# More combined feed-forward pairs, with their weight sums and input combinations made elsewhere

## The chip, the cores and the metric

One core of a Trainium2 chip runs the whole program in one launch. The metric is the time of an execution in microseconds, as the median of three runs. All arithmetic is float32. Matrix products go through TensorE's fp32r format, which keeps fewer bits than float32, so each operand is split in a high and a low half and each product is made three times: high x high, high x low, low x high.

## What is computed

Two transformer blocks over 512 positions of width 1024. The first: a norm, an mLSTM with four heads beside a dilated window attention with 24 heads, gates, an output projection (`out`), then a feed-forward. The second: gated linear attention beside sparse attention, `out2`, then a feed-forward. Both feed-forwards have 2816 hidden columns, that is 22 blocks of 128:

```
h = rmsnorm(x, g)                 # x * r * g, with r = rsqrt(mean(x*x) + 1e-6), one r per position
x = x + (silu(h @ w_gate) * (h @ w_up)) @ w_down      # block 2 norms the feed-forward's output before adding
```

## The kernel before

The activations lie transposed in SBUF: `XT` is 8 slabs of 128 features by 512 positions. The weights come from HBM as a fixed list of some 318 units. A unit makes one block of 128 output columns: 8 slabs of 128x128 weights against 8 slabs of 512 positions, three matmuls each, 24 matmuls of 512 columns.

One order of work is written by hand as a Python program (`program`, L1112). It is played once for each engine, with a class per engine that issues that engine's part of each step and does nothing for the rest. So each engine has one queue, in the order of the program, and the engines meet through semaphores only. SP's queue issues the loads.

`unit(e, i)` (L442) is the normal step. `ahead(e, i)` (L416) comes first: `split` of unit i+2 makes its weights' high half on ScalarE (L2064) and the low half on VectorE (L2467), for some units on GpSimd (L3267), and `load` fetches unit i+5 to one of three raw buffers `RAW`. High and low halves (`WH`, `WL`) have three buffers each. Then come the products (L1561 to L1563), then `evict`, which takes the sum out of PSUM. In the out projection `evict` is: VectorE adds the sum to XT (L2655), ScalarE makes the high half AH of XT times the norm's gain and the square, VectorE makes the low half AL (L2446), GpSimd sums the squares (L3258). The norm's factor r, spread as `RB`, is known only after all eight; so `lead` (L456) starts the first three feed-forward units (gate 0 and up 0 in turns, then gate 1) on the unscaled input, and VectorE multiplies their sums by RB when it evicts them (L2613).

From block 8 on in both feed-forwards (`PAIR_FROM`) two gate units, or two up units, are made together as a **pair** by a Strassen-Winograd scheme (`ffn_pairs`, L807). The weights of the two blocks and the two halves of the depth are four chunks a11, a12, a21, a22 of 128x512; seven products replace eight. The chunks are a11, a12, a22 and four sums s1 to s4 of them. VectorE makes the sums in place in `RAW` (L2478 to L2490, `chunk_add`). A product is 12 matmuls of 256 columns (L1637 to L1639). The other side of each product is one of seven combinations of the input's position halves and depth halves, made once per feed-forward for each slab m of four: `forms_x` scales slabs m and m+4 of XT by gain and RB (L2510), `forms` makes four sums (L2523 to L2530), `forms_hi` the high halves on ScalarE (L2078), `forms_lo` the low halves, 1024 of 1792 columns on VectorE (L2536) and the rest on GpSimd (L3282). They are issued one of these pieces per half unit, while units up 1 to up 7 run. The seven products are then put together from PSUM by VectorE (L2544 to L2563); the gate goes through silu on ScalarE and is multiplied with up (L2569). Units of `down` stand between the pairs from block 8 on. In block 1's feed-forward four PSUM banks turn, and a pair takes four.

## Time and profile before

| | before |
|---|---|
| median of 3 runs | 1911.11 us (1911.08 to 1911.13) |
| span of the profiled execution, first to last instruction | 1909.1 us |
| TensorE busy | 1898.5 us, 99% |
| VectorE busy | 1255.4 us, 66% |
| ScalarE busy | 735.3 us, 39% |
| GpSimd busy | 265.1 us, 14% |
| moved by DMA | 172.77 MB, 90 GB/s |

The profiled execution has no time of its own beside its span; the runs' median is 2.0 us above the span. Busy time is the time in which an engine has an instruction running; a matmul's record is longer than its distance to the next one, for matmuls overlap. In lines of a profile, L with a number is a line of the kernel, `out<-in` names what is written and read, and what stands in brackets or behind the bar is the idle time of the engine before the instruction and what ended it. AR is the common name of a large area that many tiles share.

### The profile page before, as it was taken

Reading aid. Unit: us, or ns where it says so; the run is one execution under the profiler, and the core shown is the slowest. Engines: PE = TensorE matmul, PEld = TensorE weight load, DVE = VectorE, ACT = ScalarE, POOL = GpSimd, SP = SyncE. Lnnn points to the kernel's source line nnn. Section 1 sums busy time; section 2 is a strip of 40 time slices with the busy share of each in tenths; the row PEclk is TensorE's granted clock in tenths of the full one; section 3 lists DMA queues with packets and bytes.
Section 4 is the critical chain, followed back from the end, with each engine's and each line's share of the span. In section 5 each row is a group of like instructions: output and inputs, shape, how many; then the busy total and the mean of one; then the engine's idle time right before and its main releaser. Section 6 shows DMA issues by size and latency. Waiting matters only on the chain.

```text
span 1909.1 us, 26308 instructions
## 1 busy us (share of the span) xinstructions
PE 1898.5 (99%) x10599; PEld 1591.0 (83%) x10599; DVE 1255.4 (66%) x1894; ACT 735.3 (39%) x1265; POOL 265.1 (14%) x156
## 2 busy tenths in 40 slices
PE   9999999999999999999999999999999999999998
PEld 7788888888888888999997778877777878899998
DVE  7777543345455748777776756766776667887874
ACT  6332322233334444344435522224444354444442
POOL 0211210111111113000004001121111133100002
PEclk9999999999999999999999999999999999999999
DMA  5322233232321323233333222322121322333332
GB/s 177 102 70 85 88 86 115 89 99 67 89 67 45 115 91 104 78 106 102 114 108 103 77 67 78 100 79 65 56 67 40 116 79 87 100 100 100 100 130 81
DMA packets 53472, 172.77 MB, mean 90 GB/s; under 512 B 5963, under 2 KB 10643, under 8 KB 53352
## 3 DMA queue, kind: packets, MB, share of 16 engines
q1 hardware_dynamic: 52912, 170.66, 28.8%
q8 instruction: 84, 1.38, 0.3%
q10 hardware_dynamic: 440, 0.44, 0.1%
q14 instruction: 36, 0.29, 0.1%
HBM read 168.86 MB, written 2.22 MB: 90 GB/s over the span
## 4 chain that ended last, share of the span: by engine, by line
PE 94%; DVE 3%; ACT 1%; POOL 1%; issue 0%; DVEq 0%
PE PS L1561 22%; PE PS L1563 22%; PE PS L1562 22%; PE PS L1637 5%; PE PS L1639 5%; PE PS L1638 5%; PE PS L1983 1%; PE PS L2005 1%; PE PS L1780 1%; PE PS L1795 1%; PE PS L1961 1%; PE PS L1841 1%; PE PS L1827 1%; PE PS L1818 1%; PE PS L1748 1%; POOL XT L3338 1%
## 5 line engine op out<-in xcount | busy, mean ns | idle before, releaser
L1561 PE MATMUL PS<-HH,WH 128*128 128x512 f32 x1124 | 444.0, 395 | 0.8 <-DVE WL L2467 0.7
L1563 PE MATMUL PS<-HH,WL 128*128 128x512 f32 x1124 | 438.0, 390 | 0.0
L1562 PE MATMUL PS<-HL,WH 128*128 128x512 f32 x1124 | 437.4, 389 | 0.0
L2064 ACT ACTIVATE WH<-RAW 128x1024 fp32r<-128x1024 f32 (+2 forms) x256 | 261.1, 1020 | 336.4 <-PE PS L1563 271.4
L2467 DVE TENSOR_TENSOR WL<-RAW,WH 128x1024 fp32r<-128x1024 f32 (+2 forms) x195 | 251.2, 1289 | 113.7 <-ACT WH L2064 112.0
L1561 PE MATMUL PS<-AH,WH 128*128 128x512 f32 x816 | 323.7, 397 | 0.0
L1563 PE MATMUL PS<-AH,WL 128*128 128x512 f32 x816 | 318.1, 390 | 0.0
L1562 PE MATMUL PS<-AL,WH 128*128 128x512 f32 x816 | 317.6, 389 | 0.0
L1561 PEld LDWEIGHTS PS<-HH,WH 128*128 128x128 f32 x1124 | 211.1, 188 | 49.7 <-issue 4.2
L1563 PEld LDWEIGHTS PS<-HH,WL 128*128 128x128 f32 x1124 | 211.0, 188 | 45.1
L1562 PEld LDWEIGHTS PS<-HL,WH 128*128 128x128 f32 x1124 | 211.2, 188 | 42.2 <-issue 0.2
L3267 POOL TENSOR_TENSOR WL<-RAW,WH 128x1024 fp32r<-128x1024 f32 (+1 forms) x61 | 139.0, 2279 | 740.1 <-ACT WH L2064 740.1
L1637 PE MATMUL PS<-AR,WH 128*128 128x256 f32 x784 | 219.6, 280 | 0.0
L1639 PE MATMUL PS<-AR,WL 128*128 128x256 f32 x784 | 218.8, 279 | 0.0
L1638 PE MATMUL PS<-AR,WH 128*128 128x256 f32 x784 | 218.8, 279 | 0.0
L1561 PEld LDWEIGHTS PS<-AH,WH 128*128 128x128 f32 x816 | 153.2, 188 | 37.1 <-issue 6.5
L1563 PEld LDWEIGHTS PS<-AH,WL 128*128 128x128 f32 x816 | 153.2, 188 | 33.0
L1562 PEld LDWEIGHTS PS<-AL,WH 128*128 128x128 f32 x816 | 153.4, 188 | 30.5 <-issue 0.5
L2613 DVE TENSOR_TENSOR AR<-PS,RB 128x512 f32<-128x512 f32 (+2 forms) x117 | 84.3, 723 | 134.5 <-PE PS L1563 128.0
L2073 ACT ACTIVATE WH<-RAW 128x512 fp32r<-128x512 f32 x196 | 119.4, 624 | 93.3 <-DVE RAW L2486 36.7
L1637 PEld LDWEIGHTS PS<-AR,WH 128*128 128x128 f32 x784 | 147.2, 188 | 1.1
L1638 PEld LDWEIGHTS PS<-AR,WH 128*128 128x128 f32 x784 | 146.7, 187 | 1.1
(360 smaller groups left out, 2260.7 us busy)
## 6 DMA issues: line engine op xcount, KB each, us to landing
RAW<-wst SPq DMA_DIRECT2D x292, 512.0 KB, 3.6
RAW<-wst SPq DMA_DIRECT2D x16, 256.0 KB, 2.6
RAW<-wst SPq DMA_DIRECT2D x8, 384.0 KB, 3.1
XT<-xT SPq DMA_DIRECT2D x3, 512.0 KB, 7.3
out<-XT SPq DMA_DIRECT2D x4, 384.0 KB, 2.5
AR<-mx SPq DMA_DIRECT2D x4, 256.0 KB, 6.2
AR<-scr SPq DMA_DIRECT2D x16, 64.0 KB, 4.3
AR<-scr SPq DMA_DIRECT2D x8, 128.0 KB, 4.8
```

What stands on the lines that cost most here:

```text
L1561: T.matmul(out, wh, XH[:, k, :], start=k == 0, stop=False)
L1562: T.matmul(out, wh, XL[:, k, :], start=False, stop=False)
L1563: m = T.matmul(out, wl, XH[:, k, :], start=False, stop=k == nk - 1)
L1637: T.matmul(out, wh[:, w], xh, start=m == 0, stop=False)
L1638: T.matmul(out, wh[:, w], xl, start=False, stop=False)
L1639: t = T.matmul(out, wl[:, w], xh, start=False, stop=m == 3)
L1748: t = T.transpose(PS[:, b, q * 128:(q + 1) * 128], src[:, q * 128:(q + 1) * 128], ident())
L2064: t = A.activation(whole(WH, i, n), raw(i)[:, 0:n], ACT.Copy, scale=1.0)
L2073: t = A.activation(chunk(WH, i, c), raw_chunk(i, c), ACT.Copy, scale=1.0)
L2467: t = V.tensor_tensor(whole(WL, i, n), raw(i)[:, 0:n], f(whole(WH, i, n)), ALU.subtract)
L2613: return V.tensor_tensor(dst, src, rb, ALU.mult)
L3267: t = G.tensor_tensor(whole(WL, i, n), raw(i)[:, 0:n], f(whole(WH, i, n)), ALU.subtract)
```

## The change

1. `PAIR_FROM` becomes 2 in the first feed-forward and 6 in the second: 20 and 16 pairs, where there were 14 and 14.
2. The weight sums s1 to s4 of all 36 pairs are made ahead by GpSimd. SP loads the two units of a pair (2 x 512 KB) to a new buffer SG (two of them), GpSimd makes the four sums, SP stores them to a tensor in HBM (1 MB). A plan by unit numbers (`sums_ahead`) says when: the first feed-forward's during the mLSTM, the attention and its gates (units 17 to 94), the second's during the first feed-forward.
3. A pair's seven chunks are then loaded one by one, 256 KB each, into half buffers of RAW, each as soon as the low half of the chunk six before is made. VectorE's `chunk_add` goes.
4. The combinations are made of x times gain, without RB. The gate sums of a pair are multiplied by RB on GpSimd (`pair_factor`), go through silu, and are multiplied by RB once more on GpSimd, which stands for the factor of the up sums.
5. In the first feed-forward the four pieces of slab m are issued together behind the eviction of out unit m+4. In the second they start at once behind the lead, one piece per half unit.
6. `forms_lo` makes all 1792 columns on VectorE.

```diff
-PAIR_FROM = 8
+PAIR_FROM = {"": 2, "2": 6}
...
+def sums_ahead():
+    plan, g = {}, AT["gate", 2, 0]
+    ahead_of = {"": list(range(17, 41, 4)) + list(range(42, 57, 3)) + list(range(57, 93, 4)),
+                "2": list(range(g - 8 if PAIR_FROM["2"] < 6 else g, g + 64, 4))}
+    for sfx, at in ahead_of.items():
+        for first, n in zip(at, [n for n, i in enumerate(PAIRS) if UNITS[i][0] in ("gate" + sfx, "up" + sfx)]):
+            last = 6 if sfx else 5
+            for step, what in ((0, "load"), (2, "s1"), (3, "s2"), (3, "s4"), (last - 1, "s3"), (last, "store")):
+                plan.setdefault(first + step, []).append((what, n))
+    return plan
...
 def ahead(e, i):
...
+    sums_on(e, i)
...
     for j in range(8):
         unit(e, unit_of("out", j))
+        if j > 3:
+            for f in (e.forms_x, e.forms, e.forms_hi, e.forms_lo):
+                f("", j - 4)
...
-    forms = [(f, m) for m in range(4) for f in (e.forms_x, e.forms, e.forms_hi, e.forms_lo, e.none)]
+    forms = [(f, m) for m in range(4) for f in (e.forms_x, e.forms, e.forms_hi, e.forms_lo)] if sfx else []
...
+            def load_piece(s, i, c):
+                for key in R_BEFORE[i, c]:
+                    sp.wait_ge(*at(*key))
+                if CHUNKS[c] in SUM_AT:
+                    n, o = PAIRS.index(i), SUM_AT[CHUNKS[c]]
+                    sp.wait_ge(*at("sum", "stored", n))
+                    src = sums_d[n, :, o:o + 512]
...
+            def sum_store(s, n):
+                sp.wait_ge(*at("sum", "s3", n))
+                sp.wait_ge(*at("sum", "s4", n))
+                S.dma_start(sums_d[n, :, :], SG[:, n % 2, :]).then_inc(*sum_out[n % 2].next("sum", "stored", n))
...
             def forms_x(s, sfx, m):
                 g = "fpre2" if sfx else "ffn_g"
-                dve.wait_ge(*at("free", "spread", "n5" if sfx else "n2"))
+                dve.wait_ge(*(at("free", "spread", "n5") if sfx else at("free", "sum", unit_of("out", m + 4))))
...
                 def scaled(dst, j, a, b):
-                    return V.scalar_tensor_tensor(out=dst, in0=XT[:, j, a:b], scalar=col(g, j), in1=RB[:, a:b],
-                                                  op0=ALU.mult, op1=ALU.mult)
+                    return V.tensor_scalar(dst, XT[:, j, a:b], col(g, j), None, ALU.mult, ALU.bypass)
...
             def forms_lo(s, sfx, m):
                 a = 1792 * m
                 dve.wait_ge(*at("forms", "hi", sfx, m))
-                t = V.tensor_tensor(TL[sfx][:, a:a + 1024], TF[:, 0:1024], f(TH[sfx][:, a:a + 1024]), ALU.subtract)
+                t = V.tensor_tensor(TL[sfx][:, a:a + 1792], TF, f(TH[sfx][:, a:a + 1792]), ALU.subtract)
...
+            def sum_add(s, n, what):
+                g = SG[:, n % 2, :]
+                s2, s4, s1, s3 = (g[:, o:o + 512] for o in (0, 512, 1024, 1536))
+                if what == "s1":
+                    pool.wait_ge(*at("sum", "raw", n, 0))
+                    pool.wait_ge(*at("sum", "raw", n, 1))
+                    t = G.tensor_tensor(s1, s1, s3, ALU.add)
...
+            def pair_factor(s, i, n):
+                pool.wait_ge(*at("free", "sum", i + n))
+                pool.wait_ge(*at("free", "spread", norm_of(UNITS[i][0])))
+                t = G.tensor_tensor(GATE[n], GATE[n], RB, ALU.mult)
...
+            def pair_silu(s, i, n):
+                pool.wait_ge(*at("silu", i + n))
+                t = G.tensor_tensor(GATE[n], GATE[n], RB, ALU.mult)
```

## Rows read from the trace of the kernel before

**Rows 1.** The page: busy time of the engines (share of the span) and instructions.
```profile
PE 1898.5 (99%) x10599; PEld 1591.0 (83%) x10599; DVE 1255.4 (66%) x1894; ACT 735.3 (39%) x1265; POOL 265.1 (14%) x156
```

**Rows 2.** The page: chain that ended last, share of the span by engine.
```profile
PE 94%; DVE 3%; ACT 1%; POOL 1%; issue 0%; DVEq 0%
```

**Rows 3.** Waits of TensorE: line waited for, us in total, times, longest.
```profile
PE PS L1539 <- DVE VT L2426: 1.5, 1, 1.5
...
PE PS L1561 <- DVE WL L2467: 0.7, 1, 0.7
```

**Rows 4.** TensorE in time, first combined pair: start us, us, engine, line, count.
```profile
776.51 0.28 PE L1637 MATMUL PS<-AR,WH 128*128 128x256 f32 x1
...
786.29 0.28 PE L1639 MATMUL PS<-AR,WL 128*128 128x256 f32 x1
...
786.41 0.40 PE L1561 MATMUL PS<-HH,WH 128*128 128x512 f32 x1
```

**Rows 5.** VectorE in time, end of the out projection and the lead of block 1.
```profile
672.45 0.69 DVE L2655 TENSOR_TENSOR XT<-XT,PS 128x512 f32<-128x512 f32 x1 [0.97 <-PE PS L1563]
...
673.93 0.75 DVE L2446 SCALAR_TENSOR_TENSOR AL<-XT,COL,AH 128x512 fp32r<-128x512 f32 x1 [0.79 <-ACT AH L2048]
...
677.89 0.69 DVE L2655 TENSOR_TENSOR XT<-XT,PS 128x512 f32<-128x512 f32 x1 [0.97 <-PE PS L1563]
...
691.79 1.45 DVE L2467 TENSOR_TENSOR WL<-RAW,WH 128x1024 fp32r<-128x1024 f32 x1 [0.79 <-ACT WH L2064]
...
700.39 1.23 DVE L2467 TENSOR_TENSOR WL<-RAW,WH 128x1024 fp32r<-128x1024 f32 x1 [7.15 <-ACT WH L2064]
```

**Rows 6.** TensorE in time: first product of gate 1 in block 1.
```profile
700.35 0.39 PE L1561 MATMUL PS<-AH,WH 128*128 128x512 f32 x1
```

**Rows 7.** ScalarE and GpSimd in time: the square of out 4, its sum.
```profile
673.80 0.62 ACT L2054 ACTIVATE AR<-XT 128x512 f32<-128x512 f32 x1
...
674.50 1.34 POOL L3258 TENSOR_TENSOR AR<-AR 128x512 f32<-128x512 f32 x1 [4.10 <-ACT AR L2054]
```

**Rows 8.** VectorE in time: combinations of the first slab, as they run now.
```profile
715.37 0.48 DVE L2510 SCALAR_TENSOR_TENSOR AR<-XT,COL,RB 128x256 f32<-128x256 f32 x1
...
716.16 0.75 DVE L2510 SCALAR_TENSOR_TENSOR AR<-XT,COL,RB 128x512 f32<-128x512 f32 x1
...
717.96 0.42 DVE L2523 TENSOR_TENSOR AR<-AR,VT 128x256 f32<-128x256 f32 x1
...
719.21 0.42 DVE L2530 TENSOR_TENSOR AR<-AR 128x256 f32<-128x256 f32 x1
```

**Rows 9.** Groups by line and shape: high halves; low halves; a weight sum.
```profile
L2078 ACT ACTIVATE AR<-AR 128x1792 fp32r<-128x1792 f32 x8 | 13.6, 1696 | 4.8 <-DVE AR L2530 4.8
...
L2536 DVE TENSOR_TENSOR AR<-AR,AR 128x1024 fp32r<-128x1024 f32 x8 | 9.8, 1222 | 0.9 <-ACT AR L2078 0.6
...
L2482 DVE TENSOR_TENSOR RAW<-RAW 128x512 f32<-128x512 f32 x28 | 19.2, 685 | 0.0
```

**Rows 10.** A VectorE tensor_scalar with two SBUF sides: duration ns, min/median/max.
```profile
L2730 DVE TENSOR_SCALAR AR<-AR,COL x16: 543/547/2300, 30.1 to 200.6; 128x512 f32<-128x512 f32 x16
```

**Rows 11.** GpSimd and VectorE in time: two operations that meet.
```profile
740.70 1.87 POOL L3299 TENSOR_TENSOR AR<-AR,RB 128x512 f32<-128x512 f32 x1 [4.16 <-ACT AR L2150]
...
741.67 1.97 DVE L2467 TENSOR_TENSOR WL<-RAW,WH 128x1024 fp32r<-128x1024 f32 x1 [0.27 <-ACT WH L2064]
```

**Rows 12.** Stretches: busy us of PE, PEld, DVE, ACT, POOL; PEclk, DMA share, GB/s.
```profile
4.00:8.00 4.00, 4.00 (x13) 3.12 (x12) 2.04 (x3) 2.94 (x5) 0.00 (x0) 1.00 1.03 387
900.00:950.00 50.00, 50.00 (x360) 47.08 (x359) 40.38 (x67) 21.55 (x37) 0.00 (x0) 1.00 0.30 96
1903.00:1904.00 1.00, 0.59 (x3) 0.17 (x1) 1.00 (x1) 0.37 (x1) 0.67 (x1) 1.00 0.47 167
1908.00:1909.00 1.00, 0.00 (x0) 0.00 (x0) 0.00 (x0) 0.00 (x0) 0.00 (x0) 0.56 0.18 68
```

**Rows 13.** TensorE before 7 us: duration ns min/median/max, first and last start.
```profile
L1539 PE MATMUL PS<-VT x13: 458/631/792, 1.5 to 6.8; 128*128 128x256 f32 x13
```

More of the change, by code:

```diff
@@ L231 @@
 R_SLOT, R_BEFORE = place_raw()
+PAIRS = [i for i in range(len(UNITS)) if pair_start(i) == i]
+SUM_AT = {"s2": 0, "s4": 512, "s1": 1024, "s3": 1536}
+def sums_ahead():
[8 more added lines that the diff above has]
+    return plan
+SUMS_AHEAD = sums_ahead()
 class Signal:
@@ L420, in ahead, with sums_on @@
     decays_on(e)
-    if i + 5 < len(UNITS):
+    if i + 5 < len(UNITS) and pair_start(i + 5) is None:
         e.load(i + 5)
+    sums_on(e, i)
+def sums_on(e, i):
+    for what, n in SUMS_AHEAD.get(i, []):
+        if what == "load":
+            e.sum_load(n)
+        elif what == "store":
+            e.sum_store(n)
+        else:
+            e.sum_add(n, what)
 def quarter(e, i, q):
@@ L804, in pair_steps, with __init__, on, lo @@
     return steps
+class Loads:
+    def __init__(self, e, at, end, chunks):
+        self.e = e
+        self.behind = {("lo", i) if c is None else ("lo", i, c) for i, c in chunks}
+        self.pieces = [(i, c) for i in range(at + 1, end) for c in (
+            ([None] if i > at + 4 else []) if pair_start(i) is None else range(7) if pair_start(i) == i else [])]
+        self.on()
+    def on(self):
+        while self.pieces and not any(x in self.behind for x in R_BEFORE.get(self.pieces[0], [])):
+            i, c = self.pieces.pop(0)
+            if c is None:
+                self.e.load(i)
+            else:
+                self.e.load_piece(i, c)
+    def lo(self, chunks):
+        for i, c in chunks:
+            self.e.chunk_lo(i, c)
+            self.behind.discard(("lo", i) if c is None else ("lo", i, c))
+            self.on()
 def ffn_pairs(e, sfx, at):
@@ L814, in ffn_pairs @@
     beyond = len(UNITS) if sfx else end + 2
[L815 removed]
+    chunks = [(i, c) for i in range(at + 2 - (pair_start(at + 1) is not None), beyond) for c in ([None] if pair_start(i) is None else
                                                               range(7) if pair_start(i) == i else [])]
[L817 to L820 removed]
+    loads = Loads(e, at, len(UNITS) if sfx else end + 5, chunks)
+    forms = [(f, m) for m in range(4) for f in (e.forms_x, e.forms, e.forms_hi, e.forms_lo)] if sfx else []
+    per_step = 1 if PAIR_FROM[sfx] > 4 else 2
+    n_hi, pending, queue = 0, [], []
     for n, (kind, i, x) in enumerate(steps):
+        if (x if kind == "pair" else x[0]) == 0:
+            for u in (i, i + 1) if kind == "pair" else (i,):
+                sums_on(e, u)
         if kind == "pair":
@@ L831, in ffn_pairs @@
         for what, i2, y in now:
-            if what == "silu":
+            if what == "factor":
+                e.pair_factor(i2, y)
+                queue.append(("silu", i2, y))
+            elif what == "silu":
                 e.pair_silu(i2, y)
@@ L850, in ffn_pairs @@
                 break
-        if n > 1 and forms:
-            f, m = forms.pop(0)
+        for f, m in forms[0:per_step]:
             f(sfx, m)
+        del forms[0:per_step]
         if kind == "unit":
@@ L856, in ffn_pairs @@
             if len(x) == 6:
-                for y in pending:
-                    e.chunk_lo(*y)
+                loads.lo(pending)
                 pending = []
@@ L869, in ffn_pairs @@
                 e.pair_add(i, x - 5)
-                queue.append(("silu" if gate else "hi", i, x - 5))
-    for y in pending:
-        e.chunk_lo(*y)
+                queue.append(("factor" if gate else "hi", i, x - 5))
+    loads.lo(pending)
     for y in chunks[n_hi:]:
         e.chunk_hi(*y)
-        e.chunk_lo(*y)
+        loads.lo([y])
 def last(e):
@@ L2091, in pair_silu @@
             def pair_silu(s, i, n):
-                act.wait_ge(*at("free", "sum", i + n))
+                act.wait_ge(*at("factor", i + n))
                 x = GATE[n]
@@ L2567, in pair_add @@
                     dve.wait_ge(*at("free", "sum", i + n))
[L2568 removed]
+                    dve.wait_ge(*at("silu2", unit_of("gate" + name[2:], j)))
                     t = V.tensor_tensor(GATE[n], GATE[n], UP, ALU.mult)
```

122 lines of the change are left out of this document (58 added, 64 removed).

## The prediction, made before the changed kernel ran

> **What bounds the kernel now.** I read the busy line and the 40 slices first. TensorE is busy 1898.5 of 1909.1 us; VectorE is at 66% over the whole span [rows 1]. The chain of waits says the same: 94% of it is TensorE [rows 2], and TensorE's own waits come to a few us, the longest of them 1.5 us at the very start and 0.7 us in the middle [rows 3]. So this kernel has two prices only. Matmul time taken out of TensorE comes off the end one for one. And any place where another engine comes late costs its whole lateness, for TensorE has no idle time later in which to make it good. What I have to find is how many matmuls go, and where VectorE's queue gets longer than the work that covers it. Durations are those of the profiled execution (span 1909.1 us); the median of the runs is 1911.11, 2.0 us more, which I add as it stands.
>
> **1. Fewer matmul columns.** A combined pair of units takes 7 products of 12 matmuls of 256 columns. The first one runs from 776.51 to 786.41, 9.90 us, one matmul every 0.118 us [rows 4]. Two plain units take 2 x 5.44 = 10.88 us, 5.44 being the distance of two evictions of the out projection, 672.45 and 677.89 [rows 5]. So a combined pair saves 0.98 us. There are 28 of them now (L2482 has one add for each [rows 9]); from block 2 on in the first feed-forward that is 20, from block 6 on in the second 16, 36 together: 8 more, **-7.9 us**. At 99% busy nothing hides this.
>
> **2. The combinations of the input move to the end of the out projection of block 1.** They ran in 16 pieces between the plain gate and up units. Now the first combined pair follows the fourth plain unit, and all four steps of slab m (scale, combine, high halves, low halves) are put, back to back, behind the eviction of out m+4. VectorE's queue is in order, and what stands behind them in it is the low half of the weights two units ahead, for which TensorE waits. I add up VectorE's queue from the eviction of out 4 at 672.45:
> - Four evictions. From the XT add at 672.45 to the end of the AL at 673.93 + 0.75 it is 2.23 us, with ScalarE's AH between [rows 5]: 8.9 us.
> - Four times the combinations. The three scalings take 1.54 us now (715.37 to 716.16 + 0.75) and the four small sums 1.67 (717.96 to 719.21 + 0.42) [rows 8]. Without RB the scalings are tensor_scalars; one of 512 elements takes 0.55 us [rows 10] where the old form took 0.75, so I take 1.2 for the three (between 1.2 and 1.54). Then VectorE waits for ScalarE's high halves, 1.70 us for 1792 elements [rows 9]: nothing stands between the two in the queue. Then the low halves, all 1792 on VectorE where it had 1024 for 1.22 us [rows 9]: 1792/1024 of that, 2.1, less the fixed part, 2.0. Sum 6.6 us, four times 26.4 us.
> - The low halves of four units' weights (out 7, gate 0, up 0, gate 1), 1.23 us each where nothing meets them [rows 5]: 4.9 us.
>
> Together 40.2 us: the low half of gate 1, which ended at 691.79 + 1.45 [rows 5], ends at 712.7. TensorE wants it at 700.35, when gate 0 and up 0 are through [rows 6]. That is **+12.3 us**, and VectorE doesn't wait for TensorE anywhere in these 40 us, so nothing shortens it. It shows earlier, in two steps: gate 0's low half is behind the combinations of slabs 0 and 1, some 4 us late; up 0's is behind slab 2's too, and since the lead takes gate 0 and up 0 in turns TensorE does six matmuls and stops again, for some 8 us. ScalarE's own queue stays ahead: in each round of about 10 us it has AH, the square, one weight split and the 1.70.
>
> The sums of squares add to this. GpSimd's sum for out 4 starts at 674.50, after ScalarE's square at 673.80 [rows 7], and slab 0's scaling is ready to start at 674.68. How the two engines meet is seen later: GpSimd's multiply at 740.70 takes 1.87 us, and VectorE's 1.23 us subtraction at 741.67 ends at 743.64, 1.2 us after GpSimd's end [rows 11]; they go one after the other. A tensor_scalar is in the same case: 0.55 us mostly, 2.30 once [rows 10]. So each slab may wait for up to 674.50 + 1.34 - 674.68 = 1.2 us, 0 to 4.6 us for four; I take **+3**, as the order is the same each time. The Trainium skill (SBUF — State Buffer, Practical consequences) says that a VectorE operation with two SBUF inputs, or a tensor_scalar in its two-port mode, and a GpSimd operation exclude each other for the whole instruction. By that rule the four waits would be there in full, 4.6; the trace's pair at 740.70 agrees with it.
>
> **3. TensorE's clock after the long stop.** No stop inside this trace is long enough to try it. At the end the granted clock is 1.00 in the microsecond of the last matmuls (1903) and averages 0.56 at 1908, with TensorE idle between [rows 12]: it has fallen from 2.4 to 1.2 GHz. The stop before up 0 is 8 us or more. What the lower level is like is seen in TensorE's first matmuls: 631 ns at the median, those of 256 columns, up to a start at 6.8 us [rows 13]; the combined pairs' are 280 [rows 4]. A stretch like that one, 5.3 us at half speed, costs 2.6 us; once or, with the 4 us stop before, almost twice: 0 to 4, I take **+2**. The Trainium skill (TensorE: Matmul & The Clock Gate, The HAM clock gate) has the array start cold again after such an idle time; by it the cost is there at least once.
>
> **4. The six combined pairs without a down unit between, block 1.** VectorE is busy 40.4 of 50 us where two pairs alternate with two down units [rows 12], so 24.8 us in a round of 30.7 (19.8 + 10.9). The four weight sums of each pair, eight of 0.605 us from start to start (0.685 long [rows 9]), leave it: 20.0. The downs' own share is 2 x (1.23 + 0.69) = 3.8. Two pairs in a row thus need 16.2 of 19.8 us. GpSimd gets, in the same 19.8 us, four multiplies by the norm's factor (two before and two behind the silu) and the four sums of a pair of block 2: eight operations of 1.3 us, each of which shuts VectorE's two-operand work out for up to its length. 16.2 + 10.4 = 26.6 if all of them hit; with two thirds of VectorE's work exposed and a share falling into its idle time, about 22, 2 us over in each of three rounds. The weight buffers are up to five products ahead, 7 us, but with four PSUM banks a pair's last addition must be done within two products (2.8 us) or the next pair waits. Bounds 0 and 7, **+2**. The stores and loads go the same way: seven quarter-size loads of 256 KB per pair (1.8 MB in 9.9 us, 185 GB/s) and 2.1 MB for every sum (106 GB/s) are 290 GB/s, under the 387 that the queues moved at the start [rows 12]. Near, but for 60 us, and each load has over 7 us to land. Nothing for it, inside those bounds.
>
> **5. The rest.** The weight sums before (80 adds from unit 17 to unit 94, and block 2's beside the first feed-forward) run on a GpSimd that is 14% busy [rows 1]. In the mLSTM and attention they meet chains that TensorE nearly waits for, and at the end of the first feed-forward eight of them stand between the sums of squares for the next norms. 0 to 4, **+0.7**. SP's stores wait for GpSimd's last sum; it is issued a whole unit earlier and raw loads have two units of slack, so nothing. Block 2's combinations now end one step before the first combined pair, and low halves are longer: 0 to 2, **+0.5**. VectorE saves weight sums and the late combinations of block 1; off the path, worth nothing.
>
> The first pair's first high half stands behind gate 1's silu in ScalarE's queue: **+0.3**.
>
> **Sum.** -7.9 + 12.3 + 3 + 2 + 2 + 0.7 + 0.5 + 0.3 = +12.9: 1911.1 + 12.9 = **1924 us**. Its own range: 1911.1 - 7.9 + 12.3 = 1915.5, if none of the bounded terms costs anything, to 1933 with about half of what is left of them.
>
> **Rivals.**
> - The combinations fit. For this the four slabs would have to vanish in VectorE's idle time between 672 and 715. It has 7.15 us before 700.39 [rows 5] and under 2 us in each out unit, about 13; the slabs take 26. Speaks for it: the old place cost TensorE nothing, and it frees VectorE later. Then the gain of step 1 stands, less about 2 for steps 4 and 5: 1905. Chance 0.10.
> - They fit partly, as ScalarE's 1.70 would if it lay beside other work (4 x 1.7 = 6.8 us less) and the clock held: 1911.1 - 7.9 + 5.5 + 2 = 1911, no change. Against it: the queue order leaves VectorE nothing to do in that time. Chance 0.08.
> - GpSimd becomes the second bound. Same stop at the out projection, and in the pairs of block 1 VectorE and GpSimd exclude each other so that the whole round takes 26.6 us for 19.8, and alternating with downs 24.8 - 4.8 + 13 = 33 for 30.7 in seven rounds; then 3 x 6.8 + 7 x 2.3 - 7 of slack = 29 more instead of 2, 1951, or half of it, 1937. It decides from the point at which more than two thirds of GpSimd's operations shut VectorE out. Chance 0.12, at 1937.
> - The forecast, 0.70.
>
> **Numbers.** Faster by over 0.2% (3.8 us; less than that can't be told from no change) comes from the first rival: 0.10. Within 0.2%: the second, and a sliver of the forecast's low end: 0.09. Slower: 0.81. The range to hold it 8 times in 10: 1914 to 1934.
>
> **What would show it.** Right: in TensorE's waits a line of L2467's successor (WL) as releaser, with two stops of about 4 and 8 us between out 7 and the end of up 0; in time, the chain scale, combine, ScalarE's 1.7 us, low halves once per out unit with weights' low halves behind; a granted clock under 1.00 right after. Combined pairs at 9.9 us each when nothing holds them, 36 of them. GpSimd's adds at 1.3 us alone and more beside VectorE. Wrong: no stop at gate 0 and up 0, or one under 6 us (step 2's queue); TensorE idle over 7 us in the first six pairs (step 4); low halves that don't wait for ScalarE.

## The result, and the profile after

The changed kernel takes 1953.99 us (1953.13 to 1954.46, 4 runs) where the kernel before takes 1911.12: ratio 1.0224, 95% interval 1.0209 to 1.0238. The forecast was 1924 us, slower by 12.9, with a range of 1914 to 1934. The direction is right, the size is not: 42.9 us more, and outside the range.

The first lines of the page of the changed kernel:

```profile
span 1951.3 us, 27489 instructions
...
PE 1903.2 (98%) x10887; PEld 1603.6 (82%) x10887; DVE 1313.5 (67%) x1854; ACT 748.7 (38%) x1313; POOL 559.9 (29%) x356
```

Against [rows 1] TensorE idles 48 us instead of 10.6 (span less busy time), GpSimd has twice its work, and VectorE, from which all weight sums were taken, is busier than before: 1313.5 us against 1255.4.

To place the loss I take the start of the same work in both kernels. The row of before, then those of the changed kernel (first and last start behind the comma; L1679 is block 2's first small unit, as L1587 is before; L1743 the norm behind block 2's attention; L1776 the last units):

```profile
L1587 PE MATMUL PS<-XT,AR x16: 592/618/643, 1035.3 to 1047.7; 128*64 128x512 f32 x16
```

```profile
L1679 PE MATMUL PS<-XT,AR x16: 592/618/643, 1068.4 to 1081.3; 128*64 128x512 f32 x16
...
L1743 PE MATMUL PS<-C,AR x16: 165/250/250, 1578.9 to 1580.5; 128*128 128x1 f32 x16
...
L1776 PE MATMUL PS<-AH,AR x32: 333/338/339, 1909.4 to 1931.9; 128*128 128x384 f32 x32
```

| up to | before | after | later by | of it new in this stretch, beside the columns |
|---|---|---|---|---|
| out 4's addition to XT | 672.45 | 674.46 | 2.0 | 2.0 |
| first pair, block 1 (before: end of the fourth plain unit) | 711.2 (700.35 + 2 x 5.44) | 730.2 | 19.0 | 17.0 |
| block 2's small unit | 1035.3 | 1068.4 | 33.1 | 14.1, and 5.9 for six pairs: 20.0 |
| block 2's post norm | 1545.4 | 1578.9 | 33.5 | 0.4 |
| last units | 1867.2 | 1909.4 | 42.2 | 8.7, and 2.0 for two pairs: 10.7 |

2.0 + 17.0 + 20.0 + 0.4 + 10.7 - 7.9 = 42.2, the difference of the spans. A stretch's new loss is what it adds to "later by", and what its pairs saved in columns on top. TensorE's clock fell behind the long stops; windows of the changed kernel (busy us, then the granted clock, DMA share, GB/s):

```profile
700.00:750.00 50.00, 41.60 (x247) 36.70 (x248) 31.43 (x43) 24.69 (x35) 12.86 (x10) 0.90 0.37 122
750.00:800.00 50.00, 43.35 (x334) 42.06 (x333) 36.48 (x56) 20.34 (x39) 22.22 (x16) 0.93 0.67 232
800.00:850.00 50.00, 45.41 (x327) 42.35 (x326) 40.16 (x53) 20.65 (x36) 23.06 (x15) 1.00 0.66 222
1650.00:1700.00 50.00, 43.06 (x310) 40.79 (x309) 40.02 (x61) 23.49 (x41) 12.49 (x9) 0.93 0.43 137
```

The granted clock is 0.50 from 696.32 to 709.97, from 778.24 to 785.07 and from 1658.88 to 1665.71. TensorE is busy for 14.8 us of these 27.3, so the lower clock took some 7.4 us of its work time (an estimate: half of the 14.8).

**First place, out 4 to the first pair: in size as forecast.** TensorE's matmuls behind its stops (in brackets the idle time before and its releaser), and VectorE's queue in one slab:

```profile
696.12 0.59 PE L1653 MATMUL PS<-AH,WH 128*128 128x512 f32 x1 [4.99 <-issue]
...
706.88 0.77 PE L1653 MATMUL PS<-AH,WH 128*128 128x512 f32 x1 [8.03 <-DVE WL L2558]
```

```profile
674.46 0.69 DVE L2721 TENSOR_TENSOR XT<-XT,PS 128x512 f32<-128x512 f32 x1 [0.97 <-PE PS L1655]
675.94 0.75 DVE L2537 SCALAR_TENSOR_TENSOR AL<-XT,COL,AH 128x512 fp32r<-128x512 f32 x1 [0.79 <-ACT AH L2139]
676.61 1.38 DVE L2577 TENSOR_SCALAR AR<-XT,COL 128x256 f32<-128x256 f32 x1
677.91 0.34 DVE L2577 TENSOR_SCALAR VT<-XT,COL 128x256 f32<-128x256 f32 x1
...
682.13 2.03 DVE L2602 TENSOR_TENSOR AR<-AR,AR 128x1792 fp32r<-128x1792 f32 x1 [1.77 <-ACT AR L2169]
684.07 1.22 DVE L2558 TENSOR_TENSOR WL<-RAW,WH 128x1024 fp32r<-128x1024 f32 x1
685.21 0.68 DVE L2721 TENSOR_TENSOR XT<-XT,PS 128x512 f32<-128x512 f32 x1
```

The round is 10.7 us, 685.21 less 674.46, for 5.4 us of TensorE's [rows 5]; two stops, 5.0 and 8.0 us. The profile names no releaser for the first; it ends as the next round's low half (L2558) does, at 694.81 + 1.22 = 696.03. The first scaling of each slab takes 1.38 us where its twin takes 0.34: it starts at 676.61 and ends at 677.99, and GpSimd's square sum (L3324) runs from 676.50 to 677.83.

**Second place, the six pairs.** TensorE stops again and again; here the chain of one of them through GpSimd, ScalarE and VectorE, in a fence for each engine's timeline:

```profile
744.46 1.62 POOL L3360 TENSOR_TENSOR SG<-SG 128x512 f32<-128x512 f32 x1
746.05 1.74 POOL L3371 TENSOR_TENSOR AR<-AR,RB 128x512 f32<-128x512 f32 x1
747.75 1.28 POOL L3366 TENSOR_TENSOR AR<-AR,RB 128x512 f32<-128x512 f32 x1
```

```profile
749.07 0.63 ACT L2185 ACTIVATE AR<-AR 128x512 f32<-128x512 f32 x1 [5.45 <-POOL AR L3366]
749.60 2.70 ACT L2164 ACTIVATE WH<-RAW 128x512 fp32r<-128x512 f32 x5
```

```profile
750.25 3.04 DVE L2567 TENSOR_TENSOR WL<-RAW,WH 128x512 fp32r<-128x512 f32 x2 [3.62 <-ACT WH L2164]
```

Ahead of the two multiplications on GpSimd stand three weight sums, 741.40 to 746.08, of which the last is shown. The factor (L3366) of the pair's second gate waits behind them and behind the first gate's second factor (L3371); ScalarE's silu (L2185) waits 5.45 us for it, and with it all the high halves of weights behind it (L2164); VectorE's low halves wait for those, TensorE for the low halves. Waits by line, 728 to 860 us:

```profile
ACT AR L2185 <- POOL AR L3366: 27.1, 8, 5.8
DVE WL L2567 <- ACT WH L2164: 25.0, 11, 6.2
```

TensorE's longest stops in this stretch are two of 2.93 us; this is the first, with the clock at 0.50 from 1.2 us behind it:

```profile
777.08 0.39 PE L1728 MATMUL PS<-AR,WH 128*128 128x256 f32 x1 [2.93 <-DVE WL L2567]
```

ScalarE's high halves of weights also wait for loads there, 13.6 us in seven waits; theory C below is about these.

**Third place, block 2's first pair** waits for the low halves of the last slab's combinations, which VectorE makes at 1660.67:

```profile
1660.67 2.02 DVE L2602 TENSOR_TENSOR AR<-AR,AR 128x1792 fp32r<-128x1792 f32 x1 [0.16 <-ACT AR L2169]
```

```profile
1662.75 0.58 PE L1728 MATMUL PS<-AR,WH 128*128 128x256 f32 x1 [6.79 <-DVE AR L2602]
```

### The profile page after: what moved, and what is told of

It is laid out like the page before. It is cut to its first block, busy times and chain, and to the rows that moved or that the text cites. A ratio compares the mean times of both kernels' runs of the same rounds, so it can differ in the third digit from the quotient of the medians.

```text
span 1951.3 us, 27489 instructions
## 1 busy us (share of the span) xinstructions
PE 1903.2 (98%) x10887; PEld 1603.6 (82%) x10887; DVE 1313.5 (67%) x1854; ACT 748.7 (38%) x1313; POOL 559.9 (29%) x356
## 4 chain that ended last, share of the span: by engine, by line
PE 83%; DVE 8%; issue 3%; ACT 3%; POOL 2%; DMA 0%; DVEq 0%; SPq 0%; ACTq 0%; POOLq 0%
PE PS L1653 19%; PE PS L1655 18%; PE PS L1654 18%; PE PS L1728 5%; PE PS L1730 5%; PE PS L1729 5%; DVE WL L2558 2%; PE PS L2074 1%; PE PS L2096 1%; PE PS L1871 1%; PE PS L1886 1%; PE PS L2052 1%; PE PS L1932 1%; PE PS L1918 1%; PE PS L1909 1%
## 5 line engine op out<-in xcount | busy, mean ns | idle before, releaser
L2558 DVE TENSOR_TENSOR WL<-RAW,WH 128x1024 fp32r<-128x1024 f32 (+2 forms) x179 | 240.0, 1341 | 98.0 <-ACT WH L2155 96.7
L1728 PE MATMUL PS<-AR,WH 128*128 128x256 f32 x1008 | 285.7, 283 | 19.7 <-DVE WL L2567 7.2
L1653 PE MATMUL PS<-AH,WH 128*128 128x512 f32 x720 | 287.8, 400 | 14.8 <-DVE WL L2558 9.4
L1730 PE MATMUL PS<-AR,WL 128*128 128x256 f32 x1008 | 283.2, 281 | 0.0
L1729 PE MATMUL PS<-AR,WH 128*128 128x256 f32 x1008 | 283.1, 281 | 0.0
L1655 PE MATMUL PS<-AH,WL 128*128 128x512 f32 x720 | 281.8, 391 | 0.0
L1654 PE MATMUL PS<-AL,WH 128*128 128x512 f32 x720 | 281.2, 391 | 0.0
L2567 DVE TENSOR_TENSOR WL<-RAW,WH 128x512 fp32r<-128x512 f32 x252 | 230.7, 948 | 44.4 <-ACT WH L2164 43.0
L1728 PEld LDWEIGHTS PS<-AR,WH 128*128 128x128 f32 x1008 | 191.1, 190 | 24.0 <-DVE WL L2567 7.8
L1729 PEld LDWEIGHTS PS<-AR,WH 128*128 128x128 f32 x1008 | 190.6, 189 | 1.0
L1730 PEld LDWEIGHTS PS<-AR,WL 128*128 128x128 f32 x1008 | 191.4, 190 | 0.0
L1653 PEld LDWEIGHTS PS<-AH,WH 128*128 128x128 f32 x720 | 135.7, 189 | 49.9 <-issue 21.5
L2164 ACT ACTIVATE WH<-RAW 128x512 fp32r<-128x512 f32 x252 | 148.1, 621 | 68.4 <-DMA RAW<-wst 47.2
```

Source lines behind the costliest of these rows:

```text
L1653: T.matmul(out, wh, XH[:, k, :], start=k == 0, stop=False)
L1654: T.matmul(out, wh, XL[:, k, :], start=False, stop=False)
L1655: m = T.matmul(out, wl, XH[:, k, :], start=False, stop=k == nk - 1)
L1728: T.matmul(out, wh[:, w], xh, start=m == 0, stop=False)
L1729: T.matmul(out, wh[:, w], xl, start=False, stop=False)
L1730: t = T.matmul(out, wl[:, w], xh, start=False, stop=m == 3)
```

## The experiments

Theories after the result. A: three independent places, of which the second is a chain of queues. B: the second is VectorE made slow by GpSimd, which the forecast's step 4 priced at 2. C: it is the transfers, 232 GB/s there. For the first place there are two more: the 17 us are waits between VectorE's queue and ScalarE's, or they are VectorE's own instructions.

**The order behind the outs, first try.**

```diff
+            e.forms_lo("", 3)
...
+        if j > 4:
+            e.forms_lo("", j - 5)
         if j > 3:
-            for f in (e.forms_x, e.forms, e.forms_hi, e.forms_lo):
+            for f in (e.forms_x, e.forms, e.forms_hi):
                 f("", j - 4)
```

> The changed kernel, but each slab's low halves stand on VectorE's queue behind the next out's eviction (those of the last slab behind the first third of the lead), so that VectorE no longer waits for ScalarE's high halves before it evicts. Nothing else moves; the stretch of pairs and block 2 stay. Theory A (the 17 us between out 4 and the first pair are VectorE's queue and its 1.8 us waits for ScalarE, four times): the queue from out 4 on gets 4 x 1.8 = 7 us shorter, the first pair starts about 7 to 9 us earlier than in the changed kernel (730.2), and the time is 1945 to 1948. Rival B (the queue is bound by VectorE's own instructions, which GpSimd's square sums lengthen; the waits only cover what would be waited for anyway): under 3 us, 1951 to 1954. Both: the 20 us of the stretch behind it stay.

1955.96 us (1955.29 to 1956.17), 2 us more. The edit had only moved the wait. On ScalarE the next weights' high half stands behind the combinations' in both kernels (682.00 behind 680.39 in the changed one). There VectorE made the combinations' low halves meanwhile; now it has nothing to do in that time, and its L2561 (L2558 of the changed kernel, which waited for nothing) waits 2.78 us, where the wait for ScalarE was 1.77:

```profile
694.75 1.23 DVE L2561 TENSOR_TENSOR WL<-RAW,WH 128x1024 fp32r<-128x1024 f32 x1 [2.78 <-ACT WH L2158]
```

It tells the first place's two theories nothing. The second try takes that away too (the loop over outs, with slab 3's last two pieces behind the first `ahead` of the lead):

```diff
+        ahead(e, i)
+        if j > 4:
+            e.forms_hi("", j - 5)
...
         evict(e, i)
+        if j > 4:
+            e.forms_lo("", j - 5)
+        if j > 3:
+            e.forms_x("", j - 4)
+            e.forms("", j - 4)
```

> The changed kernel, but a slab's high halves stand on ScalarE's queue behind the next weight split and not ahead of it, its low halves on VectorE's queue behind the next eviction, and the scalings and sums of the following slab behind these. Now no queue holds the other: the combinations of a slab have a whole out to pass through ScalarE. Theory A (the 17 us are waits between the two queues, each slab 1.8 us in the changed kernel, 2.8 us in the kernel before this one): 7 us go, 1945 to 1949. Theory B (they are VectorE's own instructions: from out 4 on it has 8.2 us of work in a slab and 0.8 us behind ScalarE's input halves, 9.0 us for each 5.4 us of TensorE): the period is 9.0 and not 10.7 us, which is the same 7 us, but 12 us of the 17 stay whatever the order. Both are wrong, and the place is bound otherwise, at 1951 to 1956.

1945.90 us, 8.1 less than the changed kernel. Evictions at 681.02, 690.17 and 699.29: a round of 9.1 us, as expected. So of the 17.0 us about 7 (the first pair starts at 723.3, not 730.2) were queues waiting for each other; 10 stay with VectorE's own instructions. GpSimd's square sum is among these: now it meets the combinations' low halves, which take 3.12 us where they took 2.03, and the first scaling takes 0.35.

```profile
683.16 3.12 DVE L2615 TENSOR_TENSOR AR<-AR,AR 128x1792 fp32r<-128x1792 f32 x1
```

**The order in the pairs.** In each step of `ffn_pairs`:

```diff
-        if (x if kind == "pair" else x[0]) == 0:
-            for u in (i, i + 1) if kind == "pair" else (i,):
-                sums_on(e, u)
...
             else:
                 e.pair_lo(i2, y)
+        if (x if kind == "pair" else x[0]) == 0:
+            for u in (i, i + 1) if kind == "pair" else (i,):
+                sums_on(e, u)
```

> The changed kernel, but in the stretch of pairs the sum additions of a step stand on GpSimd's queue behind the factor and the second half of silu of that step, and not ahead of them. The same instructions, the same transfers, the same amount of GpSimd beside VectorE. Theory A (the 20 us between the first pair at 730 and block 2's first unit are a chain of queues: silu on ScalarE waits up to 5.8 us for the factor, which stands behind three additions on GpSimd; behind the silu stand the weights' high halves, behind them VectorE's low halves, and then TensorE): most of it goes, 12 to 18 us, 1936 to 1942, and TensorE's stops at 751, 777 and 804 us disappear. Rival B (GpSimd's additions slow VectorE's instructions, as step 4 of the forecast had it): the work is the same, so under 3 us, 1951 to 1955. Rival C (the transfers land late): also under 3 us.

1946.59 us, 7.4 less. The stretch from the first pair to block 2 takes 330.5 us (731.3 to 1061.8) for 338.2. The longest waits of the chain are gone, the loss is not:

```profile
DVE WL L2567 <- ACT WH L2164: 12.5, 10, 2.4
```

Half of what A expected. B and C, by which nothing was to change, don't explain it. The stops at 751, 777 and 804 were to disappear; each of the three rounds has three shorter ones in their place (1.1, 0.8 and 0.7 us), and the clock doesn't fall. In the changed kernel TensorE worked 6.2 us at 0.50 behind the stop at 777, so some 3 of the 7.7 us that the stretch is shorter are the clock's (an estimate).

**The additions made short.**

```diff
-                s2, s4, s1, s3 = (g[:, o:o + 512] for o in (0, 512, 1024, 1536))
+                w = 8 if n >= len([i for i in PAIRS if i < 200]) else 512
+                s2, s4, s1, s3 = (g[:, o:o + w] for o in (0, 512, 1024, 1536))
```

> The changed kernel, but GpSimd's sum additions for block 2 (those that run in block 1's stretch of pairs) add 8 columns of 512, so block 2's weight sums are not made; all transfers, waits and queues stay. Theory A (chain of queues behind three additions of 1.6 us): the additions are short, so the chain goes whichever way they are ordered: 12 to 20 us, 1934 to 1942. Rival B (port contention between GpSimd and VectorE): the same, 12 to 20 us; only against the kernel with the factor first can the two be told apart. Rival C (the transfers, 1 MB in and 1 MB out for each pair): nothing goes, 1951 to 1955.

This kernel leaves block 2's weight sums unmade. 1937.55 us, 16.4 less, 322.3 us for the stretch: another 8.2 beyond the order. It is the additions' time, not only their place. C falls as the main cause: all transfers are still there.

**The same sums at another time.** First in block 1's downs, every third unit:

```diff
-                "2": list(range(g - 8 if PAIR_FROM["2"] < 6 else g, g + 64, 4))}
+                "2": list(range(g + 12, g + 60, 3))}
```

> The changed kernel, but block 2's sums are made from the first down unit on, every third unit, and no longer beside the six pairs that have no downs between them. The same adds and the same transfers in all, none of them (adds, 1 MB in, 1 MB out for each pair) in 731 to 810 us. Against the run with 8 columns (16.4 us less than the changed kernel) it takes the transfers out of that stretch too. Theory A (the adds cost 16 us there and the transfers nothing): 1936 to 1939. Theory B (the transfers cost the rest of the 20 us): 1932 to 1935. Rival C (the adds cost wherever they stand, and every third unit is too dense): 1942 or more.

1992.36 us, 38 more. Rival C's range (1942 or more, every third unit too dense) holds it, but its mechanism, the additions, isn't what the trace shows: I had made a new wait. SyncE's queue in that kernel:

```profile
925.39 0.43 SPq L1559 DMA_DIRECT2D sums<-SG  x1
932.09 0.81 SPq L1553 DMA_DIRECT2D SG<-wst  x2
932.95 0.90 SPq L1547 DMA_DIRECT2D RAW<-wst  x2
```

With a unit's spacing less, the load of pair n+2 follows the store of pair n into the same buffer at once, waits for it to land (ten times between 840 and 1040 us, 61.4 us in all, 6.3 at most), and the weights' pieces wait in the queue behind it. TensorE stopped 20 times for a pair's low halves between 840 and 1060, 29.2 us. A version meant to be best had the same plan, with pairs from 6 and from 8, the combinations one piece a step and the factor ahead of the sums. It was expected at 1910 to 1914 and took 1971.72 us: 15 such waits of SyncE's, 76.5 us in its whole run, where the changed kernel, with every fourth unit, has 6 and 9.5 us. No run has every third unit and a third buffer, so the 38 us aren't split between these waits and the denser additions.

Then in block 2's first half, every fourth unit (`range(AT["gv", 0, 0], AT["gv", 0, 0] + 64, 4)`):

> The changed kernel, but block 2's sums are made in block 2's own first half (behind its first small unit, every fourth unit) and not in block 1's feed-forward part. The same adds and transfers in all. Every third unit in block 1's downs cost 38 us: there SyncE's queue waited ten times, 61 us, for a store that it had issued just before, with the weights' pieces behind it. Here the spacing is four units, so a load finds its buffer's store landed. Theory A (the adds cost 16.4 us beside the pairs, transfers a little more, and next to nothing beside mLSTM and attention, where block 1's sums cost 0.9): 1934 to 1938. Rival B (adds and transfers cost their price wherever they stand): 1948 to 1956.

1947.24 us, 6.7 less. Block 2's small unit starts at 1052.2, so the stretch of pairs takes 321.1 us, 17.1 less than in the changed kernel and 1.2 less than with short additions: the share of the transfers (and of what short additions still take). But block 2's first half took 520.7 us in place of 510.5. In 500 us of it, this kernel and the changed one:

```profile
1052.00:1552.00 500.00, 490.52 (x2744) 384.73 (x2743) 360.25 (x527) 188.46 (x368) 168.58 (x104) 1.00 0.43 142
```

```profile
1068.00:1568.00 500.00, 497.79 (x2788) 391.88 (x2788) 340.17 (x532) 191.38 (x370) 78.08 (x46) 1.00 0.25 80
```

VectorE has 20 us more to do with no more instructions. Both theories were half right: the price moves with the sums, and it is smaller there, 10 for 17. About half of the 10 is one place: TensorE stops 3.15 us before 1527.65, beside the last pair's additions, and the clock is 0.50 from 1527.99 to 1531.40. A version below with two pairs fewer has no such stop and pays 5.0 us.

In this kernel the six pairs have no sums beside them, and a gate pair and an up pair take 775.22 - 754.37 = 20.85 us, and 19.8 were forecast. Each round of seven plus seven products has one wait for VectorE's last addition into the bank that the next pair needs:

```profile
775.22 0.39 PE L1728 MATMUL PS<-AR,WH 128*128 128x256 f32 x1 [0.71 <-DVE VT L2629]
```

Three rounds make 3.1 of the 20.0 us.

**Block 2 from 8 on.** `PAIR_FROM = {"": 2, "2": 8}`.

> The changed kernel with block 2's pairs from block 8 on, as before, so that only block 1 starts earlier. Theory A (block 2's 10.7 us come from its combinations, which have to fit ahead of a first pair that starts two blocks earlier, and make TensorE stop 6.8 us at 1662.75 and run at the low level behind it): the stop goes, 10.7 us less, and two pairs become four units, 2.0 us more: 1945 (1943 to 1948). Rival B (VectorE is late in block 2 because the sums' transfers or the combinations lengthen everything there, wherever the first pair stands): 1 to 4 us stay, 1949 to 1953.

1945.86 us (1944.66 to 1948.47; the profiled execution is the slowest of the four), 8.1 less; the stop is gone (TensorE 49.64 of 50 us in 1650 to 1700). Between the post norm and the last units it takes 324.4 us (1580.4 to 1904.8) where the changed kernel takes 330.5 and before 321.8. With 2.0 for the two pairs given back, the stop and the low clock behind it cost 8.1, and 2.6 remain.

**Both from 8 on**, block 1's combinations one piece a step (`forms` filled for both blocks, the loop behind the outs taken out), `PAIR_FROM = {"": 8, "2": 8}`:

> The changed kernel with both blocks' pairs from block 8 on and block 1's combinations one piece a step beside gate and up 2 to 7, as before. What is left of the change: sums made by GpSimd through HBM, the factor behind the sums, no factor in the combinations. Theory A (all of the 50 us beside the columns comes from what starts earlier: the combinations behind the outs, the six pairs without downs, block 2's first pair): 1911 to 1915, with 1 to 2 us for the sums beside mLSTM and attention. Rival B (the way through GpSimd and HBM costs of itself, 5 us or more, wherever the pairs stand): 1916 to 1930.

1920.40 us, ratio to before 1.0048 (1.0033 to 1.0063). So 33.6 us of the 42.9 come with the earlier starts (41.5, less the 7.9 us of columns that they save), and 9.3 with the rest of the change, more than A had: 0.9 ahead of out, 3.7 up to the first pair, 2.1 to block 2, 2.5 behind it. Rival B in part.

**Low halves back to GpSimd**, first in that kernel, then in the changed one:

```diff
-                t = V.tensor_tensor(TL[sfx][:, a:a + 1792], TF, f(TH[sfx][:, a:a + 1792]), ALU.subtract)
+                t = V.tensor_tensor(TL[sfx][:, a:a + 1024], TF[:, 0:1024], f(TH[sfx][:, a:a + 1024]), ALU.subtract)
...
+                t = G.tensor_tensor(TL[sfx][:, a + 1024:a + 1792], TF[:, 1024:1792],
+                                    f(TH[sfx][:, a + 1024:a + 1792]), ALU.subtract)
```

> The kernel with both blocks' pairs from block 8 on and the combinations one piece a step (1920.4 us, 9.3 over before), with one part undone: 768 of the 1792 columns of a slab's low halves are again GpSimd's, so VectorE's instruction is 1024 columns wide. In that kernel 3.7 us were lost from out 4 to the first pair, where block 1's combinations stand, 2.5 us in block 2's, 2.1 us in the pairs with downs beside them and 0.9 us ahead of out. Theory A (the two losses beside the combinations are VectorE's 0.8 us more in each of eight slabs, in stretches where it is all but full): 4 to 6 us go, 1914.5 to 1916.5. Rival B (they are GpSimd's sums beside VectorE, which this makes denser): 0 or worse, 1919 to 1923.

> The changed kernel with only the split of the combinations' low halves undone: 1024 columns on VectorE and 768 on GpSimd, as before. Theory A (VectorE's 0.8 us a slab decides both places where the combinations are on the path): from out 4 on 4 x 0.8 = 3.2 us less, in block 2 another 3 us of the 10: 1946 to 1949. Rival B (GpSimd, which has the square sums at one place and the sums at both, is as late with its part as VectorE was): no change or worse, 1952 to 1957.

1920.36 (1918.42 to 1922.55) and 1955.53 us: nothing, and 1.5 more. Theory A was wrong both times. Behind the outs the round is 11.5 us in place of 10.7: VectorE's 0.8 us per slab are saved, but GpSimd's part stands beside the weights' low half, which takes 2.86 us in place of 1.22.

```profile
681.85 2.88 POOL L3368 TENSOR_TENSOR AR<-AR,AR 128x768 fp32r<-128x768 f32 x1 [4.34 <-ACT AR L2170]
```

```profile
682.95 2.86 DVE L2559 TENSOR_TENSOR WL<-RAW,WH 128x1024 fp32r<-128x1024 f32 x1
```

At block 2's first pair it is GpSimd that is late: TensorE stops 7.25 us for its part (L3368), where it stopped 6.79 for VectorE's. In the first of the two kernels block 2's part gained (322.7 us in place of 324.3); up to block 2 the profiled execution lost 3.3.

**Additions alone.** The kernel before, and in block 1's pairs 56 additions on GpSimd that touch a tile of their own:

```diff
             e.pair_products(sfx, i, x)
+            if not sfx and x % 2 == 0:
+                e.idle_add(i, x)
...
+                t = G.tensor_tensor(SG[:, :], SG[:, :], SG[:, :], ALU.add)
```

> The kernel before, with GpSimd additions of 128x512 on a tile of their own that nobody else reads or writes, one behind the low half of every second chunk of block 1's pairs (56 of them), and no transfer added. Theory A (GpSimd's additions lengthen VectorE's instructions, as step 4 of the forecast had it, but far more than it allowed): the low halves beside them take 850 to 1050 ns on average in place of 685 (rows 13 of the forecast's neighbours: 12 adds on VectorE stay too), VectorE, 81 per cent busy there, comes to 90 to 97 per cent, and 2 to 12 us are lost, all in block 1's pairs: 1913 to 1923. Rival B (the low halves are slowed by the weights' and sums' transfers, 245 GB/s there in place of 100): 685 to 700 ns, 1911 to 1912.

1911.05 us, ratio 1.000 (0.9991 to 1.0009). No time lost, yet the mechanism is there. VectorE's low halves of weight chunks and GpSimd's additions, 800 to 1000 us, in the kernel before (the first fence; there VectorE also makes 48 weight sums, in four groups like the second row), in this one, and in the changed kernel:

```profile
L2499 DVE TENSOR_TENSOR WL<-RAW,WH 128x512 fp32r<-128x512 f32 x84 | 54.6, 685 | 0.1
...
L2478 DVE TENSOR_TENSOR RAW<-RAW 128x512 f32<-128x512 f32 x12 | 8.2, 685 | 0.0
```

```profile
L2502 DVE TENSOR_TENSOR WL<-RAW,WH 128x512 fp32r<-128x512 f32 x84 | 64.6, 802 | 0.1
...
L3289 POOL TENSOR_TENSOR SG<-SG 128x512 f32<-128x512 f32 x48 | 59.5, 1239 | 125.0 <-DVE WL L2502 125.0
```

```profile
L2567 DVE TENSOR_TENSOR WL<-RAW,WH 128x512 fp32r<-128x512 f32 x92 | 93.9, 1058 | 17.3 <-ACT WH L2164 17.2
...
L3360 POOL TENSOR_TENSOR SG<-SG 128x512 f32<-128x512 f32 x19 | 33.8, 1791 | 0.7
```

With nothing but additions the low halves go from 685 to 802 ns, and VectorE's busy time in these 200 us from 157.4 to 172.6: 0.32 us for each of the 48. Transfers had no part in it. It costs no time: VectorE was 79% busy there and is 86% now. In the changed kernel 0.37 us are added to each of 92 low halves, 34 us, where 48 weight sums of 0.685 (32.9 us) had been taken off. The work given away came back as longer instructions. Two of the runs above say whose the 0.37 are. With short additions and all transfers the low halves take 872 ns in the same 200 us:

```profile
L2567 DVE TENSOR_TENSOR WL<-RAW,WH 128x512 fp32r<-128x512 f32 x93 | 78.4, 872 | 6.3 <-ACT WH L2164 5.3
```

With the sums in block 2's first half, so neither additions nor their transfers there, they take 877. So the additions make 0.19 of the 0.37, the sums' transfers nothing that can be seen, and 0.19 stay. What is left beside VectorE then is GpSimd's 28 multiplications by the factor and the loads by chunks; how the rest divides between these wasn't measured.

VectorE's share doesn't tell where the additions cost time. These 56 stand only beside pairs that alternate with downs, and there the changed kernel's TensorE doesn't stop either: it has no stop over 0.15 us between 811 and 1024. In the pairs without downs VectorE is busy for 85% of 731 to 811 with long additions (factor first) and with short ones, and the long ones cost 8.2 us.

**Versions meant to be best.** Each is put together from the edits above, with `PAIR_FROM` as

```diff
-PAIR_FROM = {"": 2, "2": 6}
+PAIR_FROM = {"": 2, "2": 8}
```

in the first and `{"": 6, "2": 8}` in the other two. The first two have block 2's sums in its own first half; the third has them in block 1's feed-forward, at `[g - 2, g + 2] + list(range(g + 12, g + 60, 4))`.

> The changed kernel with all the repairs that leave block 1's pairs at block 2: high halves behind the next weight split (8.1 us), block 2's pairs from 8 on (8.1), factor ahead of the sums, and block 2's sums in its own first half (together some 17 to 19 of the 20 us of the pair stretch). If the places are independent, 1954 less 33 to 35: 1919 to 1921, and what is left over before, 8 to 10 us, is VectorE's own work from out 4 to the first pair. If they overlap (a later first pair hides part of the others), 1923 to 1928.

> Meant to be the best form of the idea: block 1's pairs from 6 on, block 2's from 8 on; combinations one piece a step with GpSimd's 768 columns of low halves; factor ahead of the sums; block 2's sums in block 2's own first half. Of the losses found so far there stay 0.9 us ahead of out and about as much beside block 2's first half, and up to 1 us in the combinations; two pairs more bring 0.9 us in place of 2.0 (20.85 us for a gate pair and an up pair without downs and sums beside them, measured, against four units' 21.8): 1911 to 1913, no better than before. If the combinations don't fit ahead of a first pair that starts two blocks earlier (stops on VectorE's low halves in the four units before it): 1914 to 1917.

> The best arrangement so far (1918.7 us: pairs from 6 and 8, combinations one piece a step, GpSimd's 768 columns, factor ahead of the sums), but with block 2's sums back in block 1's feed-forward part, every fourth unit, none beside the two pairs that have no downs. That one lost 1.7 us up to block 2, 5.4 us in block 2's first half and 0.9 us in its combinations. Theory A (beside downs the sums cost 2 us for all of block 1's pairs, as in the kernel with all from 8 on): 1914 to 1916. Rival B (with the factor ahead or the denser combinations they cost 6 us here as well): 1918 to 1921. In neither case less than before.

1927.88, 1918.65 (ratio 1.0039, 1.0026 to 1.0053) and 1923.78 us. All three are slower than their first theories had them. The first is 26.1 under the changed kernel. Its time lies where the expectation put places that overlap, but they don't: order and pair stretch add up nearly as measured alone (block 2's small unit starts 23.1 earlier, where 6.9 and 17.1 make 24.0), and the sums' price in block 2's first half, 5.0 us here, is what the expectation lacked. The second, expected at 1911 to 1913 or at most 1917, pays 5.4 us there against the kernel before. The third, expected at 1921 at most, is 5 above the second: block 2's small unit starts 9.5 us later, and 6.2 of these are lost before the first pair (762.1 for 755.9), where two pairs' sums stand beside the combinations. None beats the kernel before.

## Why the prediction was wrong, step by step

- **Step 1, columns: right** as it was used; 36 pairs of 9.9 us where nothing holds them. But pairs in a row without downs take 20.85 for two.
- **Steps 2 and 3, the queue behind out 4 and the clock: right.** Forecast 12.3 + 3 + 2 and 0.3 for the hand-over, 17.6; measured 17.0. Gate 1's low half was to end at 712.7 plus 3 for the square sums, and ends at 717.46, 2.0 of which came with it into out 4: 15.1 for 15.3.

```profile
716.24 1.22 DVE L2558 TENSOR_TENSOR WL<-RAW,WH 128x1024 fp32r<-128x1024 f32 x1
```

  But TensorE doesn't wait for it. Its two stops are for gate 0's and up 0's low halves, and it comes to gate 1 at 718.85, 1.4 us behind the end of gate 1's, for it worked at the lower clock; 0.5 more go up to the first pair. The 1.04 us by which each first scaling is longer (1.38 for 0.34) is the mutual exclusion that the Trainium skill (SBUF — State Buffer, Who interferes with whom) states. By it the four waits were to be 4.6 us, and the trace agrees with 4.2. The granted clock averaged 0.90 in 700 to 750. TensorE's matmuls of 512 columns were 0.427 us apart where they are 0.227 otherwise, for 5.3 us, which is 2.6 us lost. Only 1.4 of the 2.6 show in the time: the six matmuls before the 8 us stop ran in time in which up 0's low half wasn't ready. So the forecast's 17.3 for both steps is near partly by luck: it added up the wait for gate 1's low half and put the clock on top, where the two stops ahead of it and the clock are what TensorE has. The stop at 777 and block 2's, which weren't forecast, brought the lower clock back twice. One reading was off and changed nothing: VectorE's subtraction in [rows 11] ends 1.07 us behind GpSimd's multiply, not 1.2.
- **Step 4, six pairs without downs, +2 with bounds 0 and 7: this is the step that failed.** Measured 20.0: 7.7 the order on GpSimd's queue (some 3 of it by way of the clock), 8.2 the length of the additions, 1.2 the transfers, 2.9 left over, which agrees with three rounds' waits for VectorE's last addition into a bank (3.1). I summed GpSimd's and VectorE's time against a round and never followed which instruction stands behind which. `pair_factor` had put GpSimd into the chain from VectorE's addition over ScalarE's silu to the next weights, and `sums_on` ahead of it. The rival in which GpSimd is the second bound named 20.4 for this stretch and was halved to 10. Unhalved it came to 1951, 3 us from the measured time, and that is partly luck: less than half of the stretch is the length of the additions, and the 9 us that it had beside the downs are not there, where TensorE has no stop between 811 and 1024.
- **Step 5, block 2's combinations, +0.5 with bounds 0 and 2: failed too.** Measured 10.7: 8.1 the stop at the first pair and the clock behind it, 2.6 the rest. That the combinations end one step ahead of the pair was read in the program, and nothing was added up for it, though step 2's own sum (6.6 us for a slab) stood beside it.
- **Step 5, the rest, 0.7: small, but low.** 2.0 up to out 4 and 0.4 in block 2's first half.
- The clause "VectorE saves weight sums; worth nothing" was too kind: between 800 and 1000 us VectorE is busy for 166.1 us, where it was for 157.4 with the sums.

## What to carry to other kernels

Before work is moved to an idle engine, write down its queue in the places where it is needed at once, and whom each instruction keeps waiting through how many engines: here three independent additions for each pair cost 7 us in six pairs by their place alone. Count what the new work does to the instructions beside it, not only its own time: 0.3 us on VectorE for each 128x512 addition on GpSimd. Beside pairs that alternate with downs that cost no time; beside six pairs without downs the additions' length cost 8.2 us. And an edit that moves one wait should be followed into the queue that it moves it to; twice here (2.8 us on ScalarE, 6.3 us on SyncE) the experiment itself made the new one.

## What the runs showed that was not expected

GpSimd's additions of 128x512 take 1.24 us beside a VectorE that is 86% busy and 1.67 to 1.79 us in the changed kernel's pairs, where VectorE is 83% busy: the share alone doesn't set the price. In the first case each addition waits for the end of a low half of VectorE's; whether that makes the difference wasn't tried. A store of 1 MB followed by a load into its buffer held SyncE's whole queue for up to 6.3 us, and the kernel in which that was repeated for each pair lost more (38 us) than the stretch of six pairs had lost in the changed one (20).
